# A float32 spread of every expert pair's outputs, with other orders of the first projection, the down refills and the output stores

## What is computed

```
u = rmsnorm(h) @ w_in2                        # q, k, v of two attentions, and gates
om = moba_attention(...)                      # 256 x 512
od = diff_attention(...) * rsqrt(mean(od^2) + eps) * subln_g   # by head, 4 heads of 128
mix = (1 + tanh(..)) * (om @ w_pm) + (1 + tanh(..)) * (od @ w_pd)
h  = h + g1 * (mix @ w_out2)
x  = rmsnorm(h) * (1 + s2) + b2
for each expert e of 32 (a token has 2):
    y[token] += weight[token, e] * (silu(x @ wg[e]) * (x @ wu[e])) @ wd[e]
out = rmsnorm(h + g2 * y) * final_g
```

## Time and profile before

| | us |
|---|---|
| median of three executions | 1354.47 |
| the profiled execution, device time | 1354.05 |
| its span, first to last instruction | 1352.2 |
| TensorE busy | 1321.2 (98%) |
| VectorE busy | 637.1 (47%) |
| ScalarE busy | 271.0 (20%) |

### The profile page before, as it was taken

One profiled execution on the slowest core, in us unless ns is written; L12 is line 12 of the kernel. 1 busy time (PEld: TensorE's weight loads), 2 busy tenths in 40 slices (PEclk: granted clock), 3 DMA queues, 4 the chain that ended last, 5 costly groups with the idle time before them and its releaser, 6 DMA issues.

```text
span 1352.2 us, 18398 instructions
## 1 busy us (share of the span) xinstructions
PE 1321.2 (98%) x6910; PEld 919.0 (68%) x6910; DVE 637.1 (47%) x1384; ACT 271.0 (20%) x566; POOL 59.0 (4%) x60
## 2 busy tenths in 40 slices
PE   9999999999999999999899999999999999999997
PEld 6888888888899888888685788854334433334332
DVE  4652389998326776720521455243332233323322
ACT  2311133210203000000542431034111111111112
POOL 0002112000000111100000000000000000000001
PEclk9999999999999999999999999999999999999999
DMA  7344333333537989767543334479999999999996
GB/s 269 125 157 154 116 127 127 127 127 126 185 126 282 326 288 319 231 189 269 211 170 127 122 125 187 187 287 397 414 428 428 386 419 431 428 427 429 429 420 250
DMA packets 122208, 350.74 MB, mean 259 GB/s; under 512 B 4768, under 2 KB 66464, under 8 KB 108704
## 3 DMA queue, kind: packets, MB, share of 16 engines
q1 hardware_dynamic: 120528, 348.68, 67.8%
q10 hardware_dynamic: 1616, 1.20, 0.3%
HBM read 348.82 MB, written 1.05 MB: 259 GB/s over the span
## 4 chain that ended last, share of the span: by engine, by line
PE 81%; DMA 7%; DVE 6%; issue 2%; ACT 1%; DVEq 1%; SPq 0%; POOLq 0%; POOL 0%; ACTq 0%
PE bank L747 38%; PE bank L1194 20%; PE bank L997 6%; DMA dense<-in_w_gate 4%; PE bank L1074 4%; DMA arena<-in_w_up 3%; PE bank L1166 3%; DVE arena L1846 2%; PE bank L1290 2%; PE bank L1012 2%; DVE scratch L1860 1%; PE bank L961 1%; PE bank L949 1%; PE bank L1026 1%; PE bank L800 0%
## 5 line engine op out<-in xcount | busy, mean ns | idle before, releaser
L747 PE MATMUL bank<-hT,dense 128*128 128x256 f32 x2048 | 446.0, 380 | 1.3 <-ACT hT L1372 0.8
L747 PEld LDWEIGHTS bank<-hT,dense 128*128 128x128 f32 x2048 | 387.8, 190 | 58.4 <-issue 6.3
L1194 PE MATMUL bank<-arena,scratch 128*64 128x512 f32 x768 | 173.1, 604 | 7.2 <-DMA arena<-in_w_gate 2.8
L747 PE MATMUL bank<-arena,dense 128*128 128x256 f32 x704 | 154.9, 382 | 0.4 <-DVE arena L1922 0.4
L747 PEld LDWEIGHTS bank<-arena,dense 128*128 128x128 f32 x704 | 134.3, 191 | 20.4 <-issue 2.0
L1194 PEld LDWEIGHTS bank<-arena,scratch 128*64 128x64 f32 x768 | 55.9, 139 | 116.2 <-issue 115.8
L1194 PE MATMUL bank<-arena,hT 128*64 128x512 f32 x496 | 113.4, 595 | 0.7 <-ACT hT L1632 0.7
L1846 DVE SCALAR_TENSOR_TENSOR arena<-arena,par 128x256 f32<-128x256 f32 x240 | 97.8, 487 | 0.0
L2314 DVE TENSOR_TENSOR scratch<-scratch,bank 128x512 f32<-128x512 f32 x64 | 41.2, 684 | 93.3 <-PE bank L1290 91.9
L1194 PEld LDWEIGHTS bank<-arena,hT 128*64 128x64 f32 x496 | 35.2, 137 | 62.3 <-issue 59.7
L997 PE MATMUL bank<-region,dense 128*128 128x256 f32 x352 | 76.1, 379 | 0.0
(11 more groups left out here) (353 smaller groups left out, 1140.5 us busy)
## 6 DMA issues: line engine op xcount, KB each, us to landing
arena<-in_w_down SPq DMA_DIRECT2D x26, 2048.0 KB, 15.8
arena<-in_w_up SPq DMA_DIRECT2D x24, 2048.0 KB, 17.0
dense<-in_w_in SPq DMA_DIRECT2D x23, 2048.0 KB, 8.3
arena<-in_w_gate SPq DMA_DIRECT2D x14, 2048.0 KB, 20.2
arena<-in_w_ada SPq DMA_DIRECT2D x12, 2048.0 KB, 7.9
dense<-in_w_gate SPq DMA_DIRECT2D x12, 2048.0 KB, 20.5
dense<-in_w_ffn_up SPq DMA_DIRECT2D x22, 1024.0 KB, 7.6
arena<-in_w_up SPq DMA_DIRECT2D x12, 1024.0 KB, 16.2
```

The source lines that it names most:

```text
L747: last = mm(dst, chunk(k, m), src[:, k, :], start=k == 0, stop=k == k_n - 1)
L1194: last = mm(dst[e * CAP:(e + 1) * CAP, :], tokens(k, e), w[e][:, k, :], start=k == 0, stop=k == k_n - 1)
```

## The change

Every pair now spreads in float32 from `out_num` with `selT_whole`, as only the last one did; the two splitting operations of each half go away. TensorE computes tile 0 of `proj_m` ahead of the sums of squares. VectorE takes the reciprocal by heads, with the reading of `proj_m`'s tiles between them, and `proj_d` waits for `on_ready` chunk by chunk. `down` of pair 0 goes chunk by chunk over both halves of the columns, and its second expert's slot is refilled by four pieces in place of two. On SP pair 7 is refilled in the order u7, g8, d7; after it the order is as before. The output is stored by three transfers: SP issues the whole first 128 rows in one and a half of the others, ScalarE the last piece, behind its branch.

```diff
@@ refill_by_pieces, SP
-                told = 2 if pair == 1 else 9
+                told = 2 if pair == 1 else 11
...
-                pieces(down_slot if pair == 2 else down_slot[1:], down_in, wde, pair, 2, "down_used")
+                pieces(down_slot if pair == 2 else down_slot[1:], down_in, wde, pair, 4 if pair == 1 else 2, "down_used")
@@ rest, SP
+                r, p = 0, 1 + EARLY
+                sp.wait_ge(sem_("up_used"), v + p)
+                load_ups(p)
+                sp.wait_ge(sem_("gate_used"), v + p)
+                load_gates(r, p + 1)
+                sp.wait_ge(sem_("down_used"), v + p)
+                load_downs(p)
                 with sp.Fori(0, (NPAIR - EARLY) // 2 - 2) as i:
-                    refill_in_turn(0, i * 2 + (1 + EARLY), i * 2 + (v + 1 + EARLY))
                     refill_in_turn(1, i * 2 + (2 + EARLY), i * 2 + (v + 2 + EARLY))
-                refill_in_turn(0, NPAIR - 3, v + NPAIR - 3)
+                    refill_in_turn(0, i * 2 + (3 + EARLY), i * 2 + (v + 3 + EARLY))
@@ stores, SP
-            for c, half, ready, n in ((0, 0, "out_ready", 1), (0, 1, "rows_std", 1 + 3), (1, 1, "out_ready", 3),
-                                      (1, 0, "rows_std", 1 + 4)):
-                sp.wait_ge(sem_(ready), n)
-                sp.dma_start(out[c * P:(c + 1) * P, half * 512:(half + 1) * 512],
-                             out_t[:, c, half * 512:(half + 1) * 512]).then_inc(out_written, 16)
-            sp.wait_ge(out_written, 64)
+            sp.wait_ge(sem_("out_ready"), 1)
+            sp.wait_ge(sem_("rows_std"), 1 + 3)
+            sp.dma_start(out[0:P, :], out_t[:, 0, :]).then_inc(out_written, 16)
+            sp.wait_ge(sem_("out_ready"), 3)
+            sp.dma_start(out[P:2 * P, 512:1024], out_t[:, 1, 512:1024]).then_inc(out_written, 16)
+            sp.wait_ge(out_written, 48)
@@ projections, TensorE
+            pe.wait_ge(sem_("o_read"), 4)
+            projection("proj_m", om, (0,))
             pe.wait_ge(sem_("osq_ready"), 1)
             for h in range(4):
                 last = mm(bank[4 + h // 2][:, (h % 2) * T:(h % 2 + 1) * T], ones, osq[:, h, :], start=True, stop=True)
             last.then_inc(sem_("ossq_done"), 1)
+            projection("proj_m", om, (1, 2, 3))
+            projection("proj_d", od, range(4), by_chunk("on_ready"))
@@ down, TensorE
+                if nth == 0:
+                    for k in range(3):
+                        columns(0, None, (k,))
+                        columns(1, None, (k,)).then_inc(sem_("first_half"), 1)
+                    columns(0, "down_half", (3,))
+                    columns(1, "down_used", (3,))
@@ spread, TensorE
-                    numbers = (upper_half(out_num[:, part]), upper_half(out_rest[:, part]), out_last[:, part])
-                    for n, x in enumerate(numbers):
-                        for c in range(TT):
-                            ins = mm(spread_bank[2 * half + c][:], selT[:, r, c * P:(c + 1) * P], x, start=n == 0, stop=n == 2)
+                    for c in range(TT):
+                        mm(spread_bank[2 * half + c][:], selT_whole[:, c * P:(c + 1) * P], out_num[:, part], start=True,
+                           stop=True).then_inc(sem_("spread_done"), 1)
@@ end of the pass, ScalarE
+                act.wait_ge(sem_("rows_std"), 1 + 4 * (b + 1))
                 return n_max if b == 0 else None
...
             further_passes(act, n_max, moe_pass)
+            act.dma_start(out[P:2 * P, 0:512], out_t[:, 1, 0:512]).then_inc(out_written, 16)
@@ reciprocals, VectorE
-            do(V.reciprocal(stat[:], stat[:]))
+            wait_all_read(dve, "gate2")
             for h in range(4):
+                part = stat[:, h * T:(h + 1) * T]
+                do(V.reciprocal(part, part))
+                stt(od[:, h, :], od[:, h, :], par("subln_g"), part, ALU.mult, ALU.mult).then_inc(sem_("on_ready"), 1)
+                if h < 2:
+                    open_proj(h)
+            for t in range(2, 4):
+                open_proj(t)
@@ read_out, VectorE
-                    own.do(tt(out_rest[:, part], out_num[:, part], upper_half(out_num[:, part]), ALU.subtract))
-                    tt(out_last[:, part], out_rest[:, part], upper_half(out_rest[:, part]), ALU.subtract
-                       ).then_inc(sem_("oute_ready"), 1)
```

More of the change, by code:

```diff
@@ L1080, in _, with projection @@
                 attend(a, lambda: some(6, KD))
+            def projection(name, src, tiles, ready=None):
+                w = v3(have(name, 0)[:], D)
+                for t in tiles:
+                    tile(name, t, 0, 4, lambda k, m: w[:, k, (2 * t + m) * P:(2 * t + m + 1) * P], src, None if t else ready)
+            pe.wait_ge(sem_("o_read"), 4)
+            projection("proj_m", om, (0,))
             pe.wait_ge(sem_("osq_ready"), 1)
@@ L1271, in down, with spread @@
                     columns(1, "down_used")
-            def spread(r, v, last=False):
+            def spread(v):
                 pe.wait_ge(sem_("selT_ready"), v + 1)
@@ L1322, in moe_pass @@
                 pair(1, v + NPAIR - 1, b, more=False, late_gate=b + 1, late_up=2 * b + 2)
-                spread(1, v + NPAIR - 1, last=True)
+                spread(v + NPAIR - 1)
                 return n_max if b == 0 else None
@@ L1637, in pair @@
                     between()
-                read_selT(r, v, last=not more)
+                read_selT(v)
                 read_hidT(v)
@@ L2172, in _, with open_proj @@
             dve.wait_ge(sem_("ostd_ready"), 1)
-            do(V.reciprocal(stat[:], stat[:]))
-            for h in range(4):
-                stt(od[:, h, :], od[:, h, :], par("subln_g"), stat[:, h * T:(h + 1) * T], ALU.mult,
-                    ALU.mult).then_inc(sem_("on_ready"), 1)
+            def open_proj(t):
+                b = wait_tile(dve, "proj_m", t)
+                stt(gates2[:, 2 * t:2 * t + 2, :], gates2[:, 2 * t:2 * t + 2, :], 1.0, v3(b[:], T), ALU.add,
+                    ALU.mult).then_inc(read_sem("proj_m", t), 1)
+            wait_all_read(dve, "gate2")
+            for h in range(4):
+                part = stat[:, h * T:(h + 1) * T]
[5 more added lines that the diff above has]
+                open_proj(t)
             dve.wait_ge(wroute_in, 16)
@@ L2326, in slot_weights, with read_out @@
                     own.do(V.tensor_reduce(w_slot[q, r:r + 1], bank[6][q, T + 3 * e:T + 3 * e + 3], AX_X, ALU.add))
-            def read_out(own, r, v, last=False):
+            def read_out(r, v):
                 for half, done in enumerate(("down_half", "down_used")):
@@ L2332, in read_out, with pair_step @@
                     ins = stt(out_num[:, part], bank[4 + half][:], w_slot[:, r:r + 1], g2_row[:, part], ALU.mult, ALU.mult)
[L2333 to L2336, removed]
-                    own.do(tt(out_rest[:, part], out_num[:, part], upper_half(out_num[:, part]), ALU.subtract))
-                    tt(out_last[:, part], out_rest[:, part], upper_half(out_rest[:, part]), ALU.subtract
-                       ).then_inc(sem_("oute_ready"), 1)
-            def pair_step(own, r, pair, v, spread_last=True, more=True, last=False):
+                    ins.then_inc(sem_("oute_ready"), 1)
+            def pair_step(own, r, pair, v, spread_last=True, more=True):
                 if spread_last:
@@ L2347, in pair_step @@
                     select(own, r, pair + 2, v + 2)
-                read_out(own, r, v, last)
+                read_out(r, v)
             def split_rows(own):
@@ L2404, in moe_pass @@
                 pair_step(own, 0, NPAIR - 2, v + NPAIR - 2, more=False)
-                pair_step(own, 1, NPAIR - 1, v + NPAIR - 1, more=False, last=True)
+                pair_step(own, 1, NPAIR - 1, v + NPAIR - 1, more=False)
                 finish_rows(own, b, v + NPAIR - 1)
```

27 lines of the change are left out of this document (7 added, 20 removed).

## The result

The changed kernel takes 1358.07 us (median of 8 runs, 1356.81 to 1359.39), the kernel before, beside it, 1353.78 (8 runs, 1352.94 to 1356.03). The ratio is 1.0029, 95% interval 1.0018 to 1.0039: slower by 0.29%, outside the range of the prediction. The profiled execution took 1357.49 with a span of 1355.4, 3.2 more than before's 1352.2.

The account below looks back on a forecast made before the run. Expert loads and TensorE were close: TensorE paced up to pair 6, then loads up to gate 14, then TensorE. Terms -2.5 - 0.3 + 1.3 + 1.5 = 0.0 gave 1354.5 us, range 1351.0 to 1357.2.

Parts of the forecast that it names:

- -2.5 (u7): Issue of pair 7's up loads: projections -2.6, six spreads +4.0, vanished wait -2.2 and slow clock -1.7 make it 2.5 us earlier.
- 0.3 (order): Pair 7's loads reordered: second dip's 0.6 to 0.8 saved, less a possible 0.5 pause; net -0.3 us, bounds 0 and -0.8.
- 1.3 (spreads): Two float32 spreads behind the gate of pair 14 lie bare on TensorE: +1.34 us, bound 1.86.
- 1.5 (tail): End of kernel: ScalarE's store waits behind its branch and lands at 1353.5, +1.5 us; bounds -0.4 and +2.4.
- +4.0 - 3.9 + 1.3 = +1.4: Float32 spreads: six before pair 7's up loads +4.0, wait 2.2 and slow clock 1.7 gone, two bare spreads +1.3.
- only eat waits: Seven spreads from pair 7's up loads to the gate of pair 14: their 4.7 us hide in 9.8 of waits and slow clocks.
- the loads may pause 0.5 there: Expert loads at pair 8's downs: pair 7's downs wait up to 1.5 us, delaying that issue and perhaps pausing loads 0.5.
- the gap: Tail: from ScalarE's branch to what follows it, taken as 2.6 us, paid after its last rows and before its store.
- The one on the other side: Rival in the experts: TensorE becomes the bound, so the gate of pair 14 starts without a wait; +4.0, 1358.5 us, chance 0.08.
- The fall at the new stand: Rival in `proj_d`: TensorE's clock falls at its new stall, one price of 1.7, 1356.2 us; chance 0.13.
- The free tail: Rival at the end: no gap behind ScalarE's branch, the tail costs nothing, 1353.0 us; chance 0.17.
- the whole 3.8 of the projections: Rival: projections gain 3.8 for 2.6, loads 0.8 for 0.3, tail as summed; 1352.8 us, chance 0.08.

## Why the prediction was wrong

Forecast: -2.5 (u7) - 0.3 (order) + 1.3 (spreads) + 1.5 (tail) = 0.0. The two profiled spans give -1.95, +1.61, +1.90 and +1.64 = +3.2. The medians say +4.3, and the interval of the ratio is 2.4 to 5.3.

The medians by part, in us, from the differences of the ratios; their intervals reach about 1.3 to either side where a part stands alone, and about 2 where it is undone:

| part | forecast | undone | alone |
|---|---|---|---|
| projections | -2.6 | -1.5 | -1.8 |
| float32 spreads | +4.0 - 3.9 + 1.3 = +1.4 | +3.1 | +3.0 |
| order of pair 7's loads | -0.3 | -0.5 | -0.8 |
| stores | +1.5 | +1.5 | +1.8 |

- **The step that failed is the price of the float32 spread:** that seven of them up to gate 14 "only eat waits", and 0.67 for each. It costs 3.0 to 3.1 where the terms of the sum hold 1.4. Part of it is the size: "I take 3.44, 0.67 more a pair, upper bound 0.93", though its own product of rows gave 3.47; it is 3.63 and 0.86. The earlier trace rows had this very operation at 3.70, and I preferred a product of records of another form, as if full rate were reached. That is 0.4 to 0.6 behind gate 14 (1.71 in the kernel with spreads alone, 1.90 in the changed one, for 1.34) and 1.2 ahead of u7.
- **The passage from u7 to gate 14** was to give 0.3 ("the loads may pause 0.5 there. Net -0.3") and cost 1.6: 209.52 before, 211.13 after. The same stretch in all profiled executions, with the break in it (how much later than 4.89 behind the one ahead the first load of d7 or d8 lands):

| spreads, order | u7's issue to gate 14 | break |
|---|---|---|
| bfloat16, old | 209.52, 209.67, 210.11 | 0.9, 1.5, 1.8 |
| bfloat16, new | 208.65, 210.60, 210.90 | 0.1, 2.0, 1.9 |
| float32, old | 210.49, 210.70 | 2.1, 2.3 |
| float32, new | 210.18, 210.83, 210.86, 211.13, 211.31 | 1.3, 2.1, 2.0, 2.3, 2.6 |

By the means, float32 spreads go with 0.8 more (210.6 for 209.8), in the old order, and the new order with 0.3 more on top of them; the rest of the 1.6 is scatter, since four of the five in the last row are one and the same program up to gate 14 and differ by 1.1. TensorE did not run out of spare, since gate 14 still waited 1.05 to 1.11 in all seven; the time was lost in the loads. The wait for d7 came as foretold (1.42 of "up to 1.5") and held up the issue of d8, but this is not shown to be the cause: with bfloat16 spreads d8 was issued just as late (2.51 ahead of the landing of the load before it, in the changed kernel 2.43) and the break was 0.1, and with the old order there is no wait and the break stays. How a float32 spread lengthens the break, the traces don't show.
- **u7** came to 1076.00 where 1075.4 was foretold. The mechanism held: -2.73 from the projections, six spreads +5.1, the wait of 2.23 and smaller ones of 0.3 gone, and the slow clock gone (8.96 to 7.13 from the start of the up to the issue). The kernel with the spread alone, too, had neither. That it came so near has luck in it: of the 2.73, 1.7 is a fall of the clock that this one execution of the kernel before had.
- **The projections** were right in kind and, for this pair of executions, in size (2.73 for 2.6; the stand 0.87 for 1.0). As a gain in the median 2.6 was too much: 1.7 of it is a fall of the clock that came in only two of five executions with the old order. The runs give 1.5 and 1.8.
- **The tail** was right by cancellation: the gap 3.54 for 2.6, landing 2.1 for 3.0. The 2.6 was read from a branch behind which ScalarE was still busy; the moved store waits for the last rows first, and there the branch takes 3.5.
- **The rivals.** The one on the other side, at 1358.5, has nearly the time that came, but not its mechanism: it wanted gate 14 without a wait. The fall at the new stand never came. The free tail is refuted; the whole 3.8 of the projections too.

The Trainium skill (FP8 and Floating Point Precision, TensorE Precision Notes) counts four passes for a float32 product. The ratio it gives, 16 to 12, is 1.33; the trace has 3.63 to 2.77, 1.31, and agrees. The Trainium skill (Runtime: NRT & Kernel Launch, Instruction fetch mechanics) states that a taken branch out of the fetched window stalls for the fetch. The trace agrees: 3.5 with the branch, 0.04 without it. In the changed kernel packets of instructions move between the branch (1349.38) and the store (1352.89), the first at 1351.29; for which engine, the trace doesn't say.

What stays open: why the break in the loads is longer with float32 spreads, and so different between executions of one program, and what decides whether the clock falls behind a wait of 1.9 to 2.2.

## What to carry to other kernels

Where loads and the engine that frees their slots are nearly level, waits hide added work only if the loads keep their times, so price such work by a run with it alone. Look at when the loads land, one after the other: where they set the pace, the difference between two kernels stands in a few long steps. If the trace holds the very operation that a change multiplies, its own row is the price, above any product of other rows. A store put on a second queue behind a branch pays for the branch, and one without it lands no earlier than four from one queue.

## What the runs showed of the hardware that I had not expected

- Behind a stand of 1.9 to 2.4 us TensorE's clock fell to half in some executions and not in others, at the same place: after 1.94 or 1.95 before gate 14 (kept up before, fell with the projections alone), after 1.90 or 1.91 near 644 (six of thirteen). A fall costs 1.7 and moves whole medians by no more than a part of it. Among the experts no fall was seen behind a wait of 1.65 or less.
- From ScalarE's branch to what follows it are 3.5 when the engine has nothing left to do there (five executions), and 2.5 to 2.9 when its last rows still run (seven).
- Loads of 2048 KB land 4.89 apart, 428 GB/s, for 200 us; the one break in them is between 0.1 and 2.6 us long, and differs by 1.3 between executions of one program.
- Three stores issued within 0.6 us of each other land after 3.0, 3.4 and 4.0; the one issued 3.6 behind the others lands after 2.1.
